# A two-layer encoder step on one core: products that nobody reads, issued by TensorE ahead of thirteen of its waits

## What is computed

```python
for l in range(DEPTH):                                    # DEPTH = 2
    o, new_p = token_mix(rms_norm(xp, ln_attn[l]), pos_p, None, *lw)
    xp = xp + o
    xp = xp + channel_mix(rms_norm(xp, ln_ffn[l]), l, *fw)   # dense for l = 0, experts for l = 1
    ...                                                   # the same for the 32 rows xs, with caches
# token_mix: z = h @ w_in; q, k, v of group A from z; q_b = cq @ w_uq; kv = ckv @ w_ukv;
#   scores, softmax, probabilities @ v, for both groups; concat(o_a, o_b) @ w_o
# swiglu:    (silu(h @ wg) * (h @ wu)) @ wd, D_FF = 2816
# moe:       logits = h @ router; top_k 2 of 8; softmax of the two; sum of gate * swiglu of the expert
```

## Time and profile before

| | |
|---|---|
| median of 3 runs | 1350.65 us (1350.45 to 1350.69) |
| the profiled execution's own time | 1352.1 us |
| its span, first to last instruction | 1350.3 us |
| mean granted clock of TensorE over the span | 0.967 |
| PE busy | 1285.0 us, 95% of the span |
| DVE busy | 944.2 us, 70% |
| ACT busy | 805.0 us, 60% |
| DMA | 356.18 MB, mean 264 GB/s |

### The profile page before, as it was taken

One profiled execution on the slowest core, in us unless ns is written; L12 is line 12 of the kernel. 1 busy time (PEld: TensorE's weight loads), 2 busy tenths in 40 slices (PEclk: granted clock), 3 DMA queues, 4 the chain that ended last, 5 costly groups with the idle time before them and its releaser, 6 DMA issues.

```text
span 1350.3 us, 18566 instructions
## 1 busy us (share of the span) xinstructions
PE 1285.0 (95%) x6907; PEld 1050.5 (78%) x6907; DVE 944.2 (70%) x920; ACT 805.0 (60%) x798; POOL 153.6 (11%) x136
## 2 busy tenths in 40 slices
PE   5978989999989999999999999999999999999994
PEld 3457579999985567688888888888888888888883
DVE  1647344444425656388898898898888988988985
ACT  2446334333323455167787777777867877877774
POOL 3011000000000010020040120120310400301402
PEclk9978989999999989789999999999999999999997
DMA  8251085544150441589999999999999999999995
GB/s 306 52 118 33 1 262 172 159 158 162 57 183 0 98 116 40 218 288 335 374 386 372 374 394 369 361 410 355 377 390 359 390 374 386 384 368 374 399 405 192
DMA packets 125837, 356.18 MB, mean 264 GB/s; under 512 B 9043, under 2 KB 34355, under 8 KB 125760
## 3 DMA queue, kind: packets, MB, share of 16 engines
q1 hardware_dynamic: 121184, 341.16, 69.6%
q0 software_dynamic: 4208, 13.21, 3.3%
q10 hardware_dynamic: 400, 1.20, 0.2%
HBM read 347.51 MB, written 10.00 MB: 265 GB/s over the span
## 4 chain that ended last, share of the span: by engine, by line
PE 92%; DVE 3%; ACT 2%; issue 1%; DMA 1%; POOL 0%; ACTq 0%; SPq 0%; POOLq 0%; DVEq 0%
PE ps L1996 36%; PE ps L2016 18%; PE ps L1911 11%; PE ps L1694 8%; PE ps L1927 5%; PE ps L1804 1%; PE ps L2004 1%; PE ps L1851 1%; PE ps L1757 1%; PE ps L1969 1%; PE ps L1749 1%; PE ps L1769 1%; PE ps L1613 1%; PE ps L1681 1%; PE ps L1859 1%
## 5 line engine op out<-in xcount | busy, mean ns | idle before, releaser
L1162 DVE TENSOR_TENSOR w_lo<-ring,w_hi 128x2048 fp32r<-128x2048 f32 (+1 forms) x326 | 684.6, 2126 | 183.2 <-ACT w_hi L851 179.2
L851 ACT ACTIVATE w_hi<-ring 128x2048 fp32r<-128x2048 f32 (+1 forms) x326 | 574.7, 1783 | 221.3 <-PE ps L2016 68.6
L1996 PE MATMUL ps<-w_hi,xg_hi 128*128 128x512 f32 (+1 forms) x768 | 289.0, 376 | 0.4 <-DVE xg_lo L1549 0.4
L1996 PE MATMUL ps<-w_hi,xg_lo 128*128 128x512 f32 (+1 forms) x768 | 287.2, 374 | 0.0
L1996 PE MATMUL ps<-w_lo,xg_hi 128*128 128x512 f32 (+1 forms) x768 | 286.3, 373 | 0.0
L1996 PEld LDWEIGHTS ps<-w_hi,xg_hi 128*128 128x128 f32 x768 | 145.2, 189 | 26.4 <-issue 0.5
L1996 PEld LDWEIGHTS ps<-w_lo,xg_hi 128*128 128x128 f32 x768 | 145.0, 189 | 25.9
L1996 PEld LDWEIGHTS ps<-w_hi,xg_lo 128*128 128x128 f32 x768 | 145.3, 189 | 25.1
L2016 PE MATMUL ps<-w_hi,am_hi 128*128 128x512 f32 x352 | 138.5, 393 | 0.0
L2016 PE MATMUL ps<-w_lo,am_hi 128*128 128x512 f32 x352 | 137.2, 390 | 0.0
L2016 PE MATMUL ps<-w_hi,am_lo 128*128 128x512 f32 x352 | 137.0, 389 | 0.0
(11 more groups left out here) (299 smaller groups left out, 1432.8 us busy)
## 6 DMA issues: line engine op xcount, KB each, us to landing
ring<-in_moe_w_down SPq DMA_DIRECT2D x80, 1024.0 KB, 7.8
ring<-in_moe_w_gate SPq DMA_DIRECT2D x68, 1024.0 KB, 7.3
ring<-in_moe_w_up SPq DMA_DIRECT2D x66, 1024.0 KB, 8.9
ring<-in_moe_w_gate SPq DMA_DIRECT2D x32, 768.0 KB, 7.5
ring<-in_moe_w_up SPq DMA_DIRECT2D x32, 768.0 KB, 6.2
ring<-in_ffn_w_gate SPq DMA_DIRECT2D x11, 1024.0 KB, 5.4
ring<-in_ffn_w_up SPq DMA_DIRECT2D x11, 1024.0 KB, 5.4
ring<-in_ffn_w_down SPq DMA_DIRECT2D x10, 1024.0 KB, 5.0
```

What stands on the lines that cost most here:

```text
L851: A(hi[:, 0:size], src[:, 0:size], ACT.Copy).then_inc(hi_ready, 1)
L1162: V.tensor_tensor(lo[:, 0:size], src[:, 0:size], hi[:, 0:size].bitcast(F32), ALU.subtract).then_inc(lo_ready, 1)
L1996: ins = mm_(ps[:, b + c0 // 512, 0:c1 - c0], (xg_hi, xg_lo)[xp][:, k, :], w[wp][:, k % 2, c0:c1], start=(k == 0 and n == 0), stop=(k == KD ...
```

## The change

A helper `busy(v, n)` issues `n` products `ident` x `cst[:, 0:256]` into the PSUM place `v`, each with `start=True, stop=True`; nobody reads the result, and the step that owns the place overwrites it. A table `WAITING` gives `n` for steps of `PE_ORDER`. For the steps of the table `busy` is called behind `wait_room` and ahead of the waits for data; where `wait_room` stood behind those waits (`h`, `hf`, `s`, `p`, `o`, `to`) it is moved ahead of them. Three more calls stand outside the table: nine products at the dense part's entry, one in `pos` ahead of the last tile, and two ahead of the wait for the picked rows. Together these are 59 products at thirteen places.

```diff
--- before.py
+++ after.py
@@ -138,6 +138,9 @@
               ("x2", 2), ("sm", 6), ("od", 5), ("sm", 7), ("od", 4), ("wd", 0, 1), ("hfd", 2), ("top", 2), ("od", 6),
               ("x2", 0), ("od", 7), ("hfd", 0), ("wl", 0), ("top", 0), ("wl", 1), ("wd", 1, 0), ("hfd", 1), ("wd", 1, 1), ("hfdb", 1),
               ("rs", 1), ("top", 1), ("x2", 1)]]
+
+WAITING = [{("p", 1): 10, ("o", 1): 7, ("s", 3): 9, ("hf", 1): 5},
+           {("h", 0): 7, ("s", 2): 5, ("o", 2): 1, ("o", 7): 1, ("ro", 0): 1, ("rob", 1): 1}]
 
 IN_BANK = ("za", "wo")
 OPENS = ("h", "zc", "tc", "tq", "item", "titem", "s", "p", "o", "to", "hf", "ro")
@@ -1605,9 +1608,13 @@
             tr(ps[:, 0, 0:4 * KD], ln_rows[0:4 * KD, :], ident[0:4 * KD, 0:4 * KD]).then_inc(ln_done, 1)
             pe.wait_ge(ln_evac, 1)
 
+            def busy(v, n):
+
+                for _ in range(n):
+                    mm_(v[:, 0:2 * P], ident, cst[:, 0:2 * P], start=True, stop=True)
+
             def turn(key, src, rows):
 
-                wait_room(pe, key)
                 v = pair(key)
                 for k in range(KD):
                     ins = tr(v[:, k * P:k * P + rows], src[0:rows, k * P:(k + 1) * P], ident[0:rows, 0:rows])
@@ -1625,6 +1632,7 @@
             for l in range(DEPTH):
                 for step in PE_ORDER[l]:
                     kind, *which = step
+                    n_wait = WAITING[l].get(step, 0)
                     if kind == "hf" and l == 1:
 
                         t, = which
@@ -1649,8 +1657,11 @@
                         full(ins, key)
                     elif kind in ("h", "hf"):
                         t, = which
+                        key = (kind, l, t)
+                        wait_room(pe, key)
+                        busy(pair(key), n_wait)
                         pe.wait_ge(xn_ready, no(ROWS_X, l, ("x1" if kind == "h" else "x2", t)))
-                        turn((kind, l, t), xn[:, t, :], ROWS[t])
+                        turn(key, xn[:, t, :], ROWS[t])
                     elif kind == "za" and which[0] == 2:
 
                         key = ("za", l, 2)
@@ -1774,6 +1785,9 @@
                         typ, t, hg = GROUPS[g]
                         key = ("s", l, g)
                         k0, nk = KOFF[KEYS_OF[t][0]], sum(KROWS[KEYS_OF[t][0]:KEYS_OF[t][1]])
+                        wait_room(pe, key)
+                        v = pair(key)
+                        busy(v, n_wait)
                         if typ == "a":
                             for tt in ((0,), (0, 1), (2,))[t]:
                                 wait_out(pe, ("tq", l, tt))
@@ -1781,8 +1795,6 @@
                                 wait_out(pe, ("tc", l))
                         for n in NEEDS.get(g, ()):
                             wait_out(pe, ("titem", l, n))
-                        wait_room(pe, key)
-                        v = pair(key)
                         if t == 2:
                             for kv in range(KVH):
                                 o = v[:, 512 * kv:512 * kv + nk]
@@ -1877,6 +1892,7 @@
                     elif kind == "rob":
 
                         key = ("ro", l, 1)
+                        busy(pair(key)[:, 512:1024], n_wait)
                         wait_out(pe, ("hf", l, 1))
                         for k in range(4, KD):
                             ins = mm_(pair(key)[:, 0:NE], xT1[:, k, :], wr[:, k, :], start=False, stop=(k == KD - 1))
@@ -1887,14 +1903,17 @@
                         key = ("to", l, t)
                         for g in OF_TILE[t]:
                             wait_out(pe, ("o", l, g))
+                        wait_room(pe, key)
                         if t < 2:
                             turn(key, xn[:, t, :], P)
                             continue
-                        wait_room(pe, key)
                         for y in range(2):
                             ins = tr(pair(key)[:, P * y:P * y + P], xn[:, 2, P * y:P * y + P], ident)
                         full(ins, key)
                 if l == 0:
+                    wait_tile(pe, l, 0)
+                    wait_tile(pe, l, 1)
+                    busy(pair(("gate", 0)), 9)
                     for t in range(3):
                         wait_out(pe, ("hf", l, t))
                     pe.wait_ge(tok_ready, 3)
@@ -1939,6 +1958,8 @@
             wait_room(pe, key)
             found_first = sorted(range(3), key=lambda t: TOPS[1]["top", t])
             for n, t in enumerate(found_first):
+                if n == 2:
+                    busy(pair(key)[:, 512:1024], 1)
                 pe.wait_ge(members, n + 1)
                 r = ROWS[t]
                 for kind, name in enumerate(("upper", "ones")):
@@ -1961,6 +1982,7 @@
                     ins = tr(ps[:, 4 + k // 4, (k % 4) * P:(k % 4 + 1) * P], xr[:, k * P:(k + 1) * P], ident)
                 ins.then_inc(xgT_full, 1)
 
+            busy(pair(key)[:, 512:1024], 2)
             pe.wait_ge(pick_ready, 1)
             pe.wait_ge(xn_ready, no(ROWS_X, 1, ("x2", 1)))
             for k in range(KD):
```

## The result

The changed kernel took 1359.75 us (median of 4 runs, 1358.91 to 1361.14) against 1350.67: a ratio of 1.0066, 95% interval 1.005 to 1.0082. It is slower by 9.1 us, where 3.8 less were forecast.

A forecast was written before the change was run, and what follows sets the result against it. TensorE, 92% of the chain, was taken to bound the kernel, with 75 us at half clock. Terms summed to +4.4 us before the routing and -8.2 there: -3.8, so 1347 us; eight-in-ten range 1341 to 1359.

The forecast's parts named there:

- The mechanism of the loss: At waits for room, products behind wait_room fill nothing; they start when the step would have, and everything behind them waits.
- the routing: Gather L1969, table L1976 and first expert products: clock back some 2.5 us into the gather, -8.2 us.
- rival (a): Clock stays down in the routing; nothing won, late products cost 0.8 to 1.0: +5.4, 1356 us; chance 0.33.
- Layer 0: Products behind room waits at p 1, o 1 and s 3 add +9.7 us; bounds +3.4 to about +11.5.
- `p` 1: Layer 0: ten products behind room, 6.6 us, less about 1.3 from faster transposes: net +5.3 us.
- `o` 1: Layer 0: seven products behind room, 4.7 us, with faster work behind them: net +1.0 us.
- `s` 3: Layer 0: nine products after 4.4 us idle, 6.0 us, with faster work behind them: net +3.4 us.
- `s` 2: Layer 1: five products behind room; +1.0 if they hold the clock, about +2.8 if it falls; taken +2.3 us.
- `o` 2: Layer 1: one product may hold the clock through the half-clock stretch from 482.0: -3.0 us net, +0.4 if it fails.
- The prediction's sign for `s` 3: In the changed kernel's profile, s 3 of layer 0 should start about 11 us later than 111.25.
- The true fills: Products hidden in waits for data: hf 1 and dense entry together -2.8 us, h 0 of layer 1 -2.3 us.
- The transposes: Layer 0: transposes behind products run at full clock, against the skill's rule; by the rule the sum is 1.7 us later.

The follow-up runs named there:

- first and third experiment: Against the kernel before. First: only the 26 products at p 1, o 1, s 3 of layer 0, 1361.26 us. Third: all 59, room-wait ones ahead of room, 1337.02 us.
- the three groups alone: Only the 26 products at p 1, o 1 and s 3 of layer 0, behind wait_room, against the kernel before: 1361.26 us, ratio 1.0075.
- the true fills alone: Only products at waits for data (hf 1, dense entry, h 0, ro 0, rob, pos, picked rows), against the kernel before: 1344.33 us, ratio 0.9952.
- the kernel without products: The changed code with every count at 0, only the moved waits left, against the kernel before: 1350.98 us, ratio 1.0005.

## Why the prediction was wrong, point by point

- **The mechanism of the loss was right.** Products behind `wait_room` at a wait for room come on top of it. The first and third experiment show it from both sides: +9.9 with them alone, and a gain of 7.1 in layer 0 once they stand ahead of the room. Putting back only `p` 1's ten costs 6.0, only `s` 2's five 3.8.
- **The step that failed is the routing**, "**−8.2** (rounded down for a late return)". It measured +0.1: 0.6 late at the gather, and 0.5 given back at the experts, because the gather began later within a half-clock stretch that was again 23.9 us long. The step took it that two products at half clock and the first gathered rows would bring the clock back 2.5 us into the gather. They did not: the gather took 15.06 us, as before, in the changed kernel, and the clock stayed down too (by the mean clock) in five of six runs with all products ahead of the room. Eight did, and so did the gather by tile. This was rival (a), at 0.33; it was the case that the rows spoke for, since 15 us of these very products had not raised the clock.
- **Mis-sized terms, nearly all on the same side.** Layer 0 +11.0 for +9.7: `p` 1 cost what was forecast (+5.3), `o` 1 +1.5 for +1.0 (its seven took 4.9 us for 4.7, and 0.2 more went in the steps behind), `s` 3 +4.1 for +3.4 (its nine took 6.7 us for the 6.0 taken; what it gave back, 2.6, was as forecast). `s` 2 +3.0 for +2.3: the clock fell 0.3 us ahead of its five, and they took 3.9 us. `o` 2 −2.1 for −3.0. With them rival (a) would have been about 1359 and not 1356, and the range (up to 1359) would not have ended 0.75 us under the result. The prediction's sign for `s` 3, "about 11 us later", also falls short of its own terms (5.3, 1.0 and 6.0, or 12.3); it came 14.2 later.
- **The `o` 2 term was right by luck, as far as it was right.** Its −3.0 was to come from one product that holds the clock. But the kernels with no product there (the three groups alone, the true fills alone, `s` 2's products alone) gave 3.3, 3.2 and 2.5 us in the same part, between `s` 3 and `tq` 1 of layer 1, and taking the product out of the kernel with products ahead changed nothing. So the stretch at half clock shortened or went without that product; the profiles differ in when the work ahead of it came, and why that moves the stretch is not shown.
- **The true fills were right**: −2.8 and −2.2 for −2.8 and −2.3, and the kernel with them alone is faster.
- **The start of the program**, 0.6 us later in this profiled execution, is no part of the change: the kernel without products shows no difference, and over all the profiles the room for `p` 1 comes between 1.3 us earlier and 1.3 later than before.
- **The transposes.** The sixteen of `titem` 3 and 4 run at full clock in the changed kernel (1.95 us for 3.65), as the sum by the rows had it. The Trainium skill, TensorE: Matmul & The Clock Gate, Part 4, has it that transposes do not engage the full clock; these rows show that some 1.8 us of them did not lower it, which is little. That transposes can raise it rests on the earlier trace rows, and the kernel without products repeats it: nothing but transposes from 91.70, the clock back at 95.20. In the 34 us at half clock above, transposes stand among other work and do not raise it.

What stays open: `s` 2's cost in the kernel before, beyond the 1.4 us of one profile; why the clock stays down in layer 0 in some runs; and why one change of place moves the stretches at half clock far behind it. The products ahead of the room also went to other banks. The same banks behind the room were not tried, so that the banks alone make no difference is argued from the timelines, where the products simply start with the gap or behind it.

## What to carry to other kernels

Before filling a wait with idle work, ask what ends it: if it is room in the place that the idle work writes, the work starts when the wait ends and lies on the path in full (here 18.4 us of products in layer 0, of which the faster steps behind gave back some 7); give it a place of its own that is empty, ahead of the wait. Keeping a clock up pays where slow work follows a gap, and the dose counts: two products ahead of the gather bought nothing, eight bought 5 us. Here the thin stretch was better made dense (like shapes in a row, ratio 0.9838) than padded (0.9871). And a gain behind an edit is not the edit's until a run without it lacks the gain.

## What the runs showed of the hardware

- Changing the number of rows from product to product costs time. Gathered column by column (32, 128, 128 rows) 48 records took 8.51 us with the clock up, by tile 5.82; at half clock they took 15.06. The first order has 15 changes between 32 and 128 rows and the second one, so a change costs some 0.19 us at full clock (2.69 us over 14). The single records say the same: behind a change, in either direction, two records follow at 0.20 to 0.21 us, all others at 0.11.
- TensorE can stay at half clock for long though busy. In the profiled run with `s` 2's products alone it was busy 33.4 of 34.1 us, with transposes and products of 64 and 96 rows or 64 columns, at a granted clock of 0.50; over the same 34.1 us the kernel before ran at 0.92 and did 196 products and transposes where this run did 130. So the 3.6 to 5.1 us that the prediction took from three places are no bound for such work.
- The clock's course varies from run to run of one kernel, and with it the time: 1329.64 to 1339.5 us at mean clocks of 0.992 to 0.983 with the products ahead of the room. The Trainium skill, TensorE: Matmul & The Clock Gate, Part 1, states that the number of slow products at a kernel's start differs from run to run; no run here looks at a kernel's start, but these show the like in the middle of one (the routing's clock probably came back in one run of six).
